# Branch products of a parallel mixer layer: two output blocks as seven block products

## The chip, the core and the metric

One core of one Trainium2 chip runs the kernel. The metric is the device time of one execution in microseconds (us). The kernel before takes 1344.15 us (median of three runs, 1344.06 to 1344.16).

## What is computed

One layer of an encoder on two groups of 512 tokens with the same weights, 1024 channels. Three attention branches A, B and C each give a state of 512 channels. The part that matters here is the merge of the three branches:

```
gates = jax.nn.sigmoid(mg).reshape(b, s, 3, D_MODEL)
m = gates[:, :, 0] * (ya @ wa) + gates[:, :, 1] * (yb @ wb) + gates[:, :, 2] * (yc @ wc)
x = x + rms_norm(m @ w_out, post_g)
```

Here `mg` is a product of the normed input with 3072 columns of the input weights, `ya`, `yb` and `yc` are the states, and `wa`, `wb`, `wc` are 512 x 1024. Everything is float32.

## The kernel before

Both groups are worked on together: 1024 tokens, channels on the partitions. TensorE multiplies numbers that are split in two parts, a rounded one (hi) and the rest (lo), and every product of two matrices is three matmuls: hi times hi, hi times lo, lo times hi. A matmul is a 128 x 128 block of weights against 128 x 512 numbers.

A weight block travels as follows. The queue of SyncE (SP) loads it from memory into one of the two slots of `stage` (`load_w`); ScalarE (ACT) writes the rounded part to `w_hi` (`split_w` at L1464); GpSimd (POOL) writes `stage` minus `w_hi` to `w_lo` (`split_w` at L666) and counts up `w_ready`; TensorE (PE) waits for that count. SP loads a block only when the split before it is done, and ACT writes a slot of `w_hi` only when PE is done with the block that was there. Blocks have numbers in one list over the whole program; a merge has sixteen of them, from `N_MERGE[b]`.

There are three merges, b = 0, 1, 2, one after each branch's attention. A merge alternates eight gate products and eight branch products. Gate product f (`merge_gate`, 48 matmuls at L843) makes 128 of the 1024 channels of a gate from the input; ACT takes its tanh. Branch product f (`merge_branch`, 24 matmuls at L1240: four blocks of 128 channels of the state, three parts, two groups) makes 128 channels of the projected state in banks 2 and 3 of PSUM (block 6: banks 0 and 1). VectorE (DVE) multiplies gate and product (`merge_add`, L2141 for b = 0; L2144 and L2146 for b = 1, 2, where it also adds to `m`) and counts up `merged`, which PE waits for before it writes these banks again. The order on PE is gate 0, gate 1, branch 0, gate 2, branch 1, gate 3, and so on; the last two are branch 6 and branch 7. The state's hi and lo parts, `y_hi` and `y_lo`, lie in `pt_hi` and `pt_lo`; DVE writes the lo part in `split_y` (L1981) just before a merge.

The order on each engine is the order of its code; nothing is scheduled. Behind merge 0 PE projects the first query block of branch B (`B_HEAD`, 24 matmuls at L1084, weights `N_B`) and then waits for `merged` before the first scores. Behind merge 1 it projects queries and keys of branch C (`N_C` and `N_C + 1`, 48 matmuls each at L843). Behind merge 2 comes the output projection (L1394). In merge 0, PE turns `rope_buf` (eight transposes at L870) ahead of branch 6.

Of the kernel before, what the change touches and what calls it, by code (L numbers as in the profile page):

```python
# [144 lines left out]
N_MERGE = [19, 42, 74]  # L145
N_B = 35
# [13 lines left out]
def build_program(nc, w_qkvg_a, w_qg_b, w_qkvg_c, w_gates, w_branch, w_out, w_pg, w_pe,  # L160
# [3 lines left out]
    with ExitStack() as ctx:  # L164
        def sb(name, shape, dt=F32):
            return ctx.enter_context(nc.sbuf_tensor(name, shape, dt))

        def sem(name):
            return ctx.enter_context(nc.semaphore(name))
# [7 lines left out]
        y = sb("y", [P, UNITS, TOK])  # L177
        q_hi = sb("q_hi", [P, TOK], F32R)
        q_lo = sb("q_lo", [P, TOK], F32R)
        k_hi = sb("k_hi", [P, TOK], F32R)  # L180
        k_lo = sb("k_lo", [P, TOK], F32R)
        v_hi = sb("v_hi", [P, TILES, 3 * HD], F32R)
        v_lo = sb("v_lo", [P, TILES, 3 * HD], F32R)
        vg = sb("vg", [P, TOK])
# [3 lines left out]
        tables = sb("tables", [P, 2 * NBIAS + ZW])  # L188
# [5 lines left out]
        spare = sb("spare", [P, TOK])  # L194
# [112 lines left out]
        merged = sem("merged")  # L307
        dve_step = sem("vector_step")
# [60 lines left out]
        v_plain_c = spare[:, 0:SEQ]  # L369

# [126 lines left out]
        def _(sp):  # L497
# [12 lines left out]
            def load_merge_rest(b):  # L510
                n = N_MERGE[b]
                with sp.Fori(0, KC - 2) as f:
                    load_w(n + 2 + 2 * f, n % 2, one(w_branch, b * KC + f))
                    load_w(n + 3 + 2 * f, (n + 1) % 2, one(w_gates, b * KC + 2 + f))
                for f in range(2):
                    load_w(n + 14 + f, (n + f) % 2, w_branch[b * KC + 6 + f])
# [87 lines left out]
            sp.wait_ge(maxed, LEAD + 24 * UNITS)  # L604
            for k in range(EARLY):
# [35 lines left out]
        def _(pool):  # L641
# [7 lines left out]
            for signal in (raw_used, bias_ready, x_pow, head_pow, y_pow, r_pow, b_pow, b_added, b_roped, w_ready, pool_step):  # L649
                pool.sem_inc(signal, LEAD)  # L650
# [17 lines left out]
            def split_merge(b, chunks):  # L668

                n, slot = N_MERGE[b], N_MERGE[b] % 2  # L670
                with pool.Fori(chunks.start, chunks.stop) as f:
                    split_w(n + 3 + 2 * f, 1 - slot)
                    split_w(n + 4 + 2 * f, slot, width=512)


# [46 lines left out]
            split_merge(0, range(1, KC - 2))  # L722
            split_w(N_MERGE[0] + 15, 0, width=512)
# [30 lines left out]
            split_merge(1, range(0, KC - 2))  # L754
            split_w(N_MERGE[1] + 15, 1, width=512)
# [40 lines left out]
            split_merge(2, range(0, KC - 2))  # L796
# [26 lines left out]
        def _(pe):  # L823
# [9 lines left out]
            for signal in (f_turned, x_turned, first_half, half_done, va_turned, rope_turned, bh_done, b_turned, b_back, scores, p_turned, p0_turned, mixed,  # L833
# [392 lines left out]
            def merge_branch(b, f, n, slot):  # L1226
# [5 lines left out]
                else:  # L1232
                    pe.wait_ge(merged, LEAD + b * KC + 1)
# [10 lines left out]

            def merge_rest(b):
# [1431 lines left out]
```

## Time and profile before

| what | us |
|---|---|
| median of three runs | 1344.15 |
| time of the profiled execution | 1343.39 |
| its span, first to last instruction | 1341.4 |
| PE busy, 6684 matmuls | 1322.7 |
| DVE busy | 602.4 |
| ACT busy | 551.9 |
| POOL busy | 301.7 |

The span leaves out what lies around the program, 2.0 us here. Busy time of PE is modelled at the end of each matmul, so the distance from one start to the next says more than a duration: a matmul is listed with 0.39 us, and the next one starts earlier than that.

### The profile page before, as it was taken

What the parts mean: (1) busy time and instruction counts of PE and PEld (TensorE: products, weight loads), DVE (VectorE), ACT (ScalarE), POOL (GpSimd) and SP (SyncE); (2) the same over time, 40 slices, a digit from 0 to 9 for tenths busy, and PEclk for the clock granted to TensorE, in tenths of its full rate; (3) what the DMA queues carried; (4) which work ended last, traced back from release to release, by engine and by line L of the source; (5) the groups of instructions that cost most, each with busy time, mean ns of one, the idle gap of its engine ahead of it and who ended that gap; (6) DMA issues with size and microseconds to landing.
All of it is one profiled execution on the core that took longest, in us unless ns stands there. A gap on an engine that the chain in (4) does not pass through costs nothing.

```text
span 1341.4 us, 17676 instructions
## 1 busy us (share of the span) xinstructions
PE 1322.7 (99%) x6684; PEld 1081.2 (81%) x6684; DVE 602.4 (45%) x1164; ACT 551.9 (41%) x1075; POOL 301.7 (22%) x199
## 2 busy tenths in 40 slices
PE   9999999999999999999999999999999999999998
PEld 6788778888888778888888888888877887888887
DVE  6355555555100477786311335555554115435222
ACT  6355554553111477676311145555553113223210
POOL 4121212221322311130222412221211222213100
PEclk9999999999999999999999999999999999999999
DMA  6111202111111100000111221111101113422111
GB/s 218 56 41 41 57 25 56 52 32 52 48 47 47 54 26 16 17 25 16 48 49 49 67 64 32 57 49 36 32 25 32 47 47 147 139 81 80 64 40 40
DMA packets 25836, 72.13 MB, mean 54 GB/s; under 512 B 2936, under 2 KB 4856, under 8 KB 25632
## 3 DMA queue, kind: packets, MB, share of 16 engines
q1 hardware_dynamic: 25760, 71.09, 16.8%
q8 instruction: 50, 0.82, 0.3%
q14 instruction: 26, 0.21, 0.0%
HBM read 66.86 MB, written 4.23 MB: 53 GB/s over the span
## 4 chain that ended last, share of the span: by engine, by line
PE 90%; DVE 4%; ACT 3%; DMA 1%; issue 1%; POOL 0%; SPq 0%; DVEq 0%; ACTq 0%; POOLq 0%
PE ps L843 18%; PE ps L862 14%; PE ps L1199 13%; PE ps L1240 9%; PE ps L1414 6%; PE ps L1084 6%; PE ps L1394 5%; PE ps L882 2%; PE ps L1021 2%; PE ps L937 2%; PE ps L1169 2%; PE ps L1420 2%; PE ps L1272 2%; PE ps L1052 1%; PE ps L1143 1%; PE ps L1119 1%
## 5 line engine op out<-in xcount | busy, mean ns | idle before, releaser
L666 POOL TENSOR_TENSOR w_lo<-stage,w_hi 128x1024 fp32r<-128x1024 f32 (+1 forms) x92 | 195.9, 2129 | 660.0 <-ACT w_hi L1464 660.0
L1464 ACT CAST w_hi<-stage 128x1024 fp32r<-128x1024 f32 (+1 forms) x92 | 86.3, 938 | 278.8 <-PE ps L843 197.6
L1981 DVE TENSOR_TENSOR pt_lo<-ps,pt_hi 128x512 fp32r<-128x512 f32 (+2 forms) x160 | 97.1, 607 | 80.5 <-ACT pt_hi L1795 40.4
L862 PE MATMUL ps<-h_hi,w_hi 128*128 128x512 f32 x272 | 110.3, 405 | 0.0
L843 PE MATMUL ps<-h_hi,w_hi 128*128 128x512 f32 x352 | 108.8, 390 | 0.0
L843 PE MATMUL ps<-h_hi,w_lo 128*128 128x512 f32 x352 | 108.4, 389 | 0.0
L843 PE MATMUL ps<-h_lo,w_hi 128*128 128x512 f32 x352 | 108.4, 389 | 0.0
L1199 PE MATMUL ps<-h_hi,w_hi 128*128 128x512 f32 x256 | 106.8, 417 | 0.0
L862 PE MATMUL ps<-h_hi,w_lo 128*128 128x512 f32 x272 | 106.2, 391 | 0.0
L862 PE MATMUL ps<-h_lo,w_hi 128*128 128x512 f32 x272 | 106.1, 390 | 0.0
L1199 PE MATMUL ps<-h_hi,w_lo 128*128 128x512 f32 x256 | 100.4, 392 | 0.0
L1199 PE MATMUL ps<-h_lo,w_hi 128*128 128x512 f32 x256 | 100.3, 392 | 0.0
L2144 DVE SCALAR_TENSOR_TENSOR s<-s,ps 128x1024 f32<-128x1024 f32 x15 | 18.3, 1220 | 149.5 <-PE ps L1240 149.5
L843 PEld LDWEIGHTS ps<-h_hi,w_lo 128*128 128x128 f32 x352 | 66.1, 188 | 13.8
L843 PEld LDWEIGHTS ps<-h_lo,w_hi 128*128 128x128 f32 x352 | 66.1, 188 | 13.8
L843 PEld LDWEIGHTS ps<-h_hi,w_hi 128*128 128x128 f32 x352 | 65.7, 188 | 14.1 <-issue 0.7
L647 POOL TENSOR_TENSOR small<-small 128x1 f32<-128x1 f32 (+3 forms) x32 | 34.1, 1067 | 173.8 <-DVE small L1996 173.0
L862 PEld LDWEIGHTS ps<-h_hi,w_hi 128*128 128x128 f32 x272 | 51.1, 188 | 15.1 <-issue 5.4
L1493 ACT ACTIVATE s<-s,stat 128x512 f32<-128x512 f32 x64 | 45.9, 719 | 38.2 <-DVE stat L2032 38.2
L1084 PE MATMUL ps<-h_hi,w_hi 128*128 128x512 f32 x144 | 59.8, 415 | 0.5 <-POOL w_lo L666 0.5
L862 PEld LDWEIGHTS ps<-h_hi,w_lo 128*128 128x128 f32 x272 | 51.1, 188 | 11.2
L1240 PE MATMUL ps<-pt_hi,w_hi 128*128 128x512 f32 x192 | 59.4, 390 | 0.0
(294 smaller groups left out, 2904.6 us busy)
## 6 DMA issues: line engine op xcount, KB each, us to landing
stage<-in_w_gates SPq DMA_DIRECT2D x24, 512.0 KB, 3.5
stage<-in_w_qkvg_a SPq DMA_DIRECT2D x19, 512.0 KB, 6.1
stage<-in_w_qkvg_c SPq DMA_DIRECT2D x16, 512.0 KB, 3.5
stage<-in_w_branch SPq DMA_DIRECT2D x24, 256.0 KB, 2.6
m<-in_x_tok SPq DMA_DIRECT2D x8, 512.0 KB, 8.2
y<-in_x_tok SPq DMA_DIRECT2D x8, 512.0 KB, 3.6
stage<-in_w_pg SPq DMA_DIRECT2D x16, 256.0 KB, 3.2
out<-y SPq DMA_DIRECT2D x16, 256.0 KB, 2.0
```

The lines of the kernel that those rows point to most:

```text
L647: nc.gpsimd.tensor_tensor(dst, src, neg_half.broadcast_to([P, n]), ALU.pow).then_inc(signal, 1)
L666: nc.gpsimd.tensor_tensor(dst, stage[:, staged, 0:width], f32(hi), ALU.subtract).then_inc(w_ready, 1)
L843: done = mm(ps[:, bank + g, :], w[:, slot, k * P:(k + 1) * P], h[:, k, g * SEQ:(g + 1) * SEQ], start=first and part == 0, stop=last and pa ...
L862: done = mm(ps[:, half_bank(T), :], w[:, slot, k * P:(k + 1) * P], h[:, k, g * SEQ:(g + 1) * SEQ], start=k == 0 and part == 0, stop=k == K ...
L1084: done = mm(ps[:, bank_b(name, unit, g), :], w[:, slot, k * P:(k + 1) * P], h[:, k, g * SEQ:(g + 1) * SEQ], start=k == 0 and part == 0, st ...
L1199: done = mm(ps[:, bank, :], w[:, slot, k * P:(k + 1) * P], h[:, k, g * SEQ:(g + 1) * SEQ], start=k == 0 and part == 0, stop=k == KC - 1 an ...
L1240: done = mm(ps[:, branch_bank(f) + g, :], w[:, slot, c * P:(c + 1) * P], yy[:, c * TOK + g * SEQ:c * TOK + (g + 1) * SEQ], start=c == 0 an ...
L1394: done = mm(ps[:, 2 * c + nb, :], a[:, k * P:(k + 1) * P], w[:, k, nb * 512:(nb + 1) * 512], start=k == 0 and part == 0, stop=k == KC - 1 ...
L1414: mm(ps[:, c, :], a[:, k * P:(k + 1) * P], w[:, k * 512:(k + 1) * 512], start=k == 0 and part == 0, stop=k == KC - 1 and part == 2)
L1464: nc.scalar.copy(dst, stage[:, staged, 0:width]).then_inc(w_hi_done, 1)
L1493: done = nc.scalar.activation(probs, probs, ACT.Exp, bias=stat[:, T % 2, 2 + e:3 + e], accum_out=stat[:, T % 2, 4 + e:5 + e])
L1981: sub = lambda out, whole, hi: nc.vector.tensor_tensor(out, whole, f32(hi), ALU.subtract)
```

## The change

Branch products of two neighbouring output blocks (a pair p: blocks 2p and 2p + 1) are made together. The pair of blocks, the two halves of the state's channels and the two groups of tokens form a 2 x 2 by 2 x 2 product, and Winograd's form of Strassen's scheme makes it of seven block products in place of eight. A block product is six matmuls (two blocks of 128 channels, three parts), so a pair is 42 matmuls in place of 48. Pairs 1, 2 and 3 are done so in merges 0 and 1, pairs 1 and 2 in merge 2 (`PAIRS`); blocks 0 and 1, and in merge 2 also 6 and 7, stay as they were. The scheme needs sums: four of the state for each merge (`state_sums` on DVE, split by ACT and by DVE in `state_lo`), four of the weights for each pair (on POOL, in `stage`, in place), and sums of the seven results (on DVE, in PSUM and in `partial`).

On PE a pair is `pair_first` (four block products into banks 0 to 3, 24 matmuls), a gate product, `pair_rest` (three block products into banks 0, 1 and 0, 18 matmuls), and a gate product; of pair 3 the two parts follow each other. SP loads both blocks of a pair with one DMA of 512 KB, where two of 256 KB were before. Loops over f are written out. Core of the diff:

```diff
+PAIRS = [range(1, KC // 2), range(1, KC // 2), range(1, KC // 2 - 1)]
+HALF_K = 2 * P
...
             def load_merge_rest(b):
...
+                for p in PAIRS[b]:
+                    sp.wait_ge(w_ready, LEAD + n + 4 * p + 1)
+                    pair = w_branch[b * KC + 2 * p:b * KC + 2 * p + 2].rearrange("a p n -> p a n")
+                    sp.dma_start(stage[:, n % 2, :].rearrange("p (a n) -> p a n", a=2), pair) \
+                        .then_inc(w_in_slot[n % 2], 16)
+                    if p < KC // 2 - 1:
+                        load_w(n + 4 * p + 3, (n + 1) % 2, w_gates[b * KC + 2 * p + 2])
+                        sp.wait_ge(w_ready, LEAD + n + 4 * p + 3)
+                        sp.sem_inc(w_in_slot[n % 2], 16)
+                        load_w(n + 4 * p + 5, (n + 1) % 2, w_gates[b * KC + 2 * p + 3])
+                    else:
+                        sp.wait_ge(w_ready, LEAD + n + 14)
+                        sp.sem_inc(w_in_slot[(n + 1) % 2], 16)
+                        sp.wait_ge(w_ready, LEAD + n + 16)
...
+            def split_pairs(b):
...
+                a11, a12, a21, a22 = [raw_w[:, q * HALF_K:(q + 1) * HALF_K] for q in range(4)]
+                split_w(n + 5, 1 - slot)
+                for p in PAIRS[b]:
+                    last = p == KC // 2 - 1
+                    pool.wait_ge(w_hi_done, LEAD + n + 4 * p + 3)
+                    steps.done(pool, nc.gpsimd.tensor_tensor(w_lo[:, slot, :], raw_w, f32(w_hi[:, slot, :]), ALU.subtract))
+                    nc.gpsimd.tensor_tensor(a22, a21, a22, ALU.add).then_inc(w_summed, 1)
...
+                    nc.gpsimd.tensor_tensor(w_lo[:, slot, 2 * HALF_K:3 * HALF_K], a22,
+                                            f32(w_hi[:, slot, 2 * HALF_K:3 * HALF_K]), ALU.subtract).then_inc(w_ready, 1)
+                    if not last:
+                        split_w(n + 4 * p + 3, 1 - slot)
+                    steps.done(pool, nc.gpsimd.tensor_tensor(a21, a11, a21, ALU.subtract))
+                    steps.done(pool, nc.gpsimd.tensor_tensor(a11, a22, a11, ALU.subtract))
+                    nc.gpsimd.tensor_tensor(a12, a12, a11, ALU.subtract).then_inc(w_summed, 1)
+                    pool.wait_ge(w_summed, LEAD + 2 * pair_number(b, p) + 2)
+                    if last:
+                        split_w(n + 15, 1 - slot, width=3 * HALF_K, staged=slot)
+                    else:
+                        split_w(n + 4 * p + 4, slot, width=3 * HALF_K)
+                        split_w(n + 4 * p + 5, 1 - slot)
...
+            def pair_first(b, p, n, slot):
+
+                pe.wait_ge(merged, LEAD + b * KC + 2 * p)
+                pe.wait_ge(w_ready, LEAD + n + 1)
+                pair_product(slot, 0, plain_state(0, 0), 0).then_inc(product_done, 1)
+                pair_product(slot, HALF_K, plain_state(1, 0), 1).then_inc(product_done, 1)
...
+            def pair_rest(b, p, n, slot):
+
+                number = pair_number(b, p)
+                pe.wait_ge(w_ready, LEAD + n + 1)
+                pe.wait_ge(p1_saved, LEAD + number + 1)
+                pair_product(slot, 0, T_PARTS[b][2], 0).then_inc(product_done, 1)
+                pe.wait_ge(bank1_used, LEAD + number + 1)
+                pair_product(slot, 2 * HALF_K, T_PARTS[b][3], 1).then_inc(product_done, 1)
+                pe.wait_ge(u2_saved, LEAD + number + 1)
+                pair_product(slot, HALF_K, plain_state(1, 1), 0).then_inc(block_done, 1)
...
+                def pair(p):
+                    number, last = pair_number(b, p), p == KC // 2 - 1
+                    raw_w = stage[:, slot, :]
+                    split_w(n + 4 * p + 2, slot, uses(4 * p + 2))
...
+                    act.wait_ge(w_summed, LEAD + 2 * number + 1)
+                    nc.scalar.copy(w_hi[:, slot, 2 * HALF_K:3 * HALF_K], raw_w[:, 3 * HALF_K:]).then_inc(s1_hi_done, 1)
...
+                        act.wait_ge(w_summed, LEAD + 2 * number + 2)
+                        split_w(n + 15, 1 - slot, uses(14), width=3 * HALF_K, staged=slot)
+                    act.wait_ge(product_done, LEAD + 4 * number + 1)
...
+                    nc.scalar.copy(partial[b][0], by_four(ps[:, 0, :])).then_inc(p1_saved, 1)
...
             merge(0)
-            split_w(N_B, 1, N_B // 2 + 1)
             act.wait_ge(rope_turned, LEAD + 2)
             q_to_hi(UNITS, 4)
+            split_w(N_B, 1, N_B // 2 + 1)
...
+                def pair(p, between_parts):
...
+                    dve.wait_ge(p1_saved, LEAD + number + 1)
+                    dve.wait_ge(product_done, LEAD + 4 * number + 2)
+                    steps.done(dve, add(bank(1), x0, bank(1)))
+                    add_quarter(2 * p, 0, 1).then_inc(bank1_used, 1)
...
+                    dve.wait_ge(product_done, LEAD + 4 * number + 3)
+                    add(x0, x0, bank(0)).then_inc(u2_saved, 1)
+                    dve.wait_ge(u2_saved, LEAD + number + 1)
+                    dve.wait_ge(product_done, LEAD + 4 * number + 4)
+                    steps.done(dve, add(x1, x0, bank(1)))
+                    add(bank(2), x1, bank(2))
+                    steps.done(dve, add(x0, x0, bank(3)))
+                    add(bank(3), x1, bank(3))
+                    dve.wait_ge(block_done, LEAD + (n + 16 if last else n + 4 * p + 5))
+                    steps.done(dve, add(bank(0), x0, bank(0)))
+                    add_quarter(2 * p, 1, 0).then_inc(merged, 1)
+                    add_quarter(2 * p + 1, 0, 2)
+                    add_quarter(2 * p + 1, 1, 3).then_inc(merged, 1)
```

`add_quarter` multiplies gate and result for 512 tokens; in merges 1 and 2 it is two instructions, of which the second adds two tiles in SBUF.

POOL at the end of merge 1 and the start of branch C, before: the body of its loop (two splits), the split for branch 7, and those for `N_C` and `N_C + 1`, behind which the bias tables of C are made.

```order
L666 TENSOR_TENSOR w_lo<-stage,w_hi 128x1024 [waits w_hi_done]
L663 REGISTER_ALU
L666 TENSOR_TENSOR w_lo<-stage,w_hi 128x512 [waits w_hi_done]
L671 REGISTER_ALU
L671 COMPARE_AND_BRANCH
L666 TENSOR_TENSOR w_lo<-stage,w_hi 128x512 [waits w_hi_done]
L666 TENSOR_TENSOR w_lo<-stage,w_hi 128x1024 [waits w_hi_done] x2
L766 TENSOR_TENSOR tables<-tables,mask 128x256 [waits raw_bias_in]
```

The same place after the change: gate 7's split, the split and the sums of pair 3, and then `N_C` and `N_C + 1`.

```order
L727 TENSOR_TENSOR w_lo<-stage,w_hi 128x1024 [waits w_hi_done]
L746 TENSOR_TENSOR w_lo<-stage,w_hi 128x1024 [waits w_hi_done]
L747 TENSOR_TENSOR stage<-stage 128x256 [waits gpsimd_step]
L750 TENSOR_TENSOR w_lo<-stage,w_hi 128x256 [waits first_weight_sum_hi_done,weight_sums_done]
L754 TENSOR_TENSOR stage<-stage 128x256
L755 TENSOR_TENSOR stage<-stage 128x256 [waits gpsimd_step]
L756 TENSOR_TENSOR stage<-stage 128x256 [waits gpsimd_step]
L727 TENSOR_TENSOR w_lo<-stage,w_hi 128x768 [waits w_hi_done,weight_sums_done]
L727 TENSOR_TENSOR w_lo<-stage,w_hi 128x1024 [waits w_hi_done] x2
L853 TENSOR_TENSOR tables_plain<-tables_plain,mask 128x256 [waits raw_bias_in]
```

The raw weights now stay in their slot of `stage` until the split of 768 columns, and `N_C` uses that slot next.

DVE at the start of merge 1, before: the lo part of the state, and then the first two outputs.

```order
L1981 TENSOR_TENSOR pt_lo<-y,pt_hi 128x1024 [waits y_hi_done] x4
L2144 SCALAR_TENSOR_TENSOR s<-s,ps 128x1024 [waits block_done,merge_tanh_done]
L2146 TENSOR_TENSOR m<-m,s 128x8x128 [waits vector_step]
L2144 SCALAR_TENSOR_TENSOR s<-s,ps 128x1024 [waits block_done,merge_tanh_done]
L2146 TENSOR_TENSOR m<-m,s 128x8x128 [waits vector_step]
```

After the change (a name with `_plain` is the same place under another type):

```order
L2146 TENSOR_TENSOR pt_lo<-y_plain,pt_hi 128x1024 [waits y_hi_done] x4
L2322 TENSOR_TENSOR k_hi_plain<-y_plain 128x512
L2323 TENSOR_TENSOR q_lo_plain<-y_plain 128x512 [waits vector_step]
L2324 TENSOR_TENSOR y_plain<-y_plain,k_hi_plain 128x512 [waits vector_step]
L2325 TENSOR_TENSOR y_plain<-y_plain 128x512 [waits vector_step]
L2322 TENSOR_TENSOR k_hi_plain<-y_plain 128x512
L2323 TENSOR_TENSOR q_lo_plain<-y_plain 128x512 [waits vector_step]
L2324 TENSOR_TENSOR y_plain<-y_plain,k_hi_plain 128x512 [waits vector_step]
L2325 TENSOR_TENSOR y_plain<-y_plain 128x512 [waits vector_step]
L2309 SCALAR_TENSOR_TENSOR s<-s,ps 128x1024 [waits block_done,merge_tanh_done]
L2311 TENSOR_TENSOR m<-m,s 128x8x128 [waits vector_step]
L2146 TENSOR_TENSOR y<-y_plain,y 128x2x512 [waits state_sums_hi_done] x2
```

Eight sums of two tiles in SBUF now stand between the state's lo part and the first output.

## Rows read from the trace of the kernel before

**Rows 1.** The page: busy time of the engines, and PE's granted clock in tenths.

```profile
PE 1322.7 (99%) x6684; PEld 1081.2 (81%) x6684; DVE 602.4 (45%) x1164; ACT 551.9 (41%) x1075; POOL 301.7 (22%) x199
...
PEclk9999999999999999999999999999999999999999
```

**Rows 2.** The chain in order of time, merge 0 and behind it: start, length, what.

```profile
335.45 5.44 PE ps L1240 x24
340.89 10.88 PE ps L843 x48
...
445.15 5.44 PE ps L1084 x24
```

**Rows 3.** Timeline of merge 0, from the end of a gate product: start, length, instruction.

```profile
335.29 0.62 PE L1240 MATMUL ps<-pt_hi,w_hi 128*128 128x512 f32 x2
335.55 1.05 ACT L1464 CAST w_hi<-stage 128x1024 fp32r<-128x1024 f32 x1 [7.14 <-PE ps L843]
...
336.67 2.40 POOL L666 TENSOR_TENSOR w_lo<-stage,w_hi 128x1024 fp32r<-128x1024 f32 x1 [12.27 <-ACT w_hi L1464]
...
339.24 0.33 SPq L501 DMA_DIRECT2D stage<-in_w_gates  x1
...
340.73 0.62 PE L843 MATMUL ps<-h_hi,w_hi 128*128 128x512 f32 x2
...
341.04 1.22 DVE L2141 SCALAR_TENSOR_TENSOR m<-s,ps 128x1024 f32<-128x1024 f32 x1 [7.40 <-PE ps L1240]
```

**Rows 4.** Groups by line and shape: instruction, count, busy us, mean ns, idle before.

```profile
L666 POOL TENSOR_TENSOR w_lo<-stage,w_hi 128x1024 fp32r<-128x1024 f32 x68 | 164.8, 2423 | 546.3 <-ACT w_hi L1464 546.3
L666 POOL TENSOR_TENSOR w_lo<-stage,w_hi 128x512 fp32r<-128x512 f32 x24 | 31.1, 1295 | 113.7 <-ACT w_hi L1464 113.7
...
L766 POOL TENSOR_TENSOR tables<-spare,mask 128x256 f32<-128x256 f32 x8 | 5.9, 735 | 0.0
...
L1464 ACT CAST w_hi<-stage 128x1024 fp32r<-128x1024 f32 x68 | 71.4, 1050 | 181.9 <-PE ps L843 161.3 <-PE ps L1240 16.5 <-DMA stage<-in_w_pe 4.1
...
L1464 ACT CAST w_hi<-stage 128x512 fp32r<-128x512 f32 x24 | 14.9, 623 | 96.9 <-PE ps L1240 60.6 <-PE ps L843 36.3
...
L1981 DVE TENSOR_TENSOR pt_lo<-ps,pt_hi 128x512 fp32r<-128x512 f32 x96 | 65.9, 687 | 42.8 <-ACT pt_hi L1795 40.4 <-ACT pt_hi L1508 2.1
...
L2330 DVE TENSOR_TENSOR tables<-tables 128x512 f32<-128x512 f32 x4 | 2.8, 689 | 0.1
```

**Rows 5.** Issues of the DMA queue: instruction, count, KB each, us to landing.

```profile
stage<-in_w_qkvg_a SPq DMA_DIRECT2D x19, 512.0 KB, 6.1
stage<-in_w_qkvg_c SPq DMA_DIRECT2D x16, 512.0 KB, 3.5
```

**Rows 6.** Timeline: PE behind a wait for DVE.

```profile
1132.95 0.70 PE L1394 MATMUL ps<-h_hi,q_hi 128*128 128x512 f32 x2 [1.83 <-DVE m L2146]
```

**Rows 7.** Timeline: DVE and POOL at work at the same time, and DVE alone.

```profile
440.93 2.41 POOL L666 TENSOR_TENSOR w_lo<-stage,w_hi 128x1024 fp32r<-128x1024 f32 x1 [5.47 <-ACT w_hi L1464]
...
441.81 1.22 DVE L2009 SCALAR_TENSOR_TENSOR q_lo<-ps,q_hi 128x1024 fp32r<-128x1024 f32 x1 [17.94 <-ACT q_hi L1467]
...
1129.34 5.72 POOL L666 TENSOR_TENSOR h_lo<-stage,h_hi 128x1024 fp32r<-128x1024 f32 x2 [7.00 <-ACT h_hi L1464]
1129.53 3.28 DVE L2146 TENSOR_TENSOR m<-m,s 128x1024 f32<-128x1024 f32 x1
...
1138.44 1.22 DVE L2146 TENSOR_TENSOR m<-m,s 128x1024 f32<-128x1024 f32 x1
```

**Rows 8.** Timeline: start of merge 1, DVE, POOL and PE.

```profile
644.34 4.62 DVE L1981 TENSOR_TENSOR pt_lo<-y,pt_hi 128x1024 fp32r<-128x1024 f32 x4
...
648.04 3.17 POOL L666 TENSOR_TENSOR w_lo<-stage,w_hi 128x1024 fp32r<-128x1024 f32 x1 [7.20 <-ACT w_hi L1464]
...
651.36 0.70 PE L843 MATMUL ps<-h_hi,w_hi 128*128 128x512 f32 x2
```

**Rows 9.** Timeline: the turn of `rope_buf` in merge 0.

```profile
433.22 1.03 PE L870 MATMUL ps<-ident,tables 128*128 128x128 f32 x8
```

More of the change, by code:

```diff
@@ L721, in _ @@
             inv_sqrt(head_rstd, head_ss, head_pow)
[L722 to L723 removed]
+            split_pairs(0)
             def split_b(k):
@@ L1243, in merge_branch, with pair_product, plain_state @@
                 done.then_inc(block_done, 1)
+            def pair_product(slot, first, state, bank):
+                hi, lo = state
+                for c in range(2):
+                    cols = slice(first + c * P, first + (c + 1) * P)
+                    for part, (w, h) in enumerate([(w_hi, hi), (w_hi, lo), (w_lo, hi)]):
+                        done = mm(ps[:, bank, :], w[:, slot, cols], h[:, c, :], start=c == 0 and part == 0,
+                                  stop=c == 1 and part == 2)
+                return done
+            def plain_state(k, g):
+                return state_half(y_hi, k, g), state_half(y_lo, k, g)
+            def pair_first(b, p, n, slot):
[3 more added lines that the diff above has]
+                pair_product(slot, HALF_K, plain_state(1, 0), 1).then_inc(product_done, 1)
+                if p == 1:
+                    pe.wait_ge(t_ready, LEAD + 4 * b + 1)
+                pair_product(slot, 3 * HALF_K, T_PARTS[b][4], 2)
+                if p == 1:
+                    pe.wait_ge(t_ready, LEAD + 4 * b + 4)
+                pair_product(slot, 2 * HALF_K, T_PARTS[b][1], 3).then_inc(block_done, 1)
+            def pair_rest(b, p, n, slot):
[7 more added lines that the diff above has]
+                pair_product(slot, HALF_K, plain_state(1, 1), 0).then_inc(block_done, 1)
             def merge_rest(b):
@@ new lines, in merge @@
+                split_w(n + 3, 1 - slot, uses(3))
+                merge_tanh(b, 1, n + 1, 1)
+                split_w(n + 4, slot, uses(4), width=512)
+                act.wait_ge(t_summed, LEAD + b + 1)
+                for k in T_ORDER[:3]:
+                    if b == 2 and k == 3:
+                        act.wait_ge(merged, LEAD + b * KC + 1)
+                    nc.scalar.copy(T_PARTS[b][k][0], T_SUMS[b][k]).then_inc(t_hi_done, 1)
+                split_w(n + 5, 1 - slot, uses(5))
+                merge_tanh(b, 2, n + 3, 0)
@@ L1706, in square_x @@
+                for p in PAIRS[b]:
+                    pair(p)
+                if KC // 2 - 1 not in PAIRS[b]:
+                    merge_tanh(b, 6, n + 11, 0)
+                    split_w(n + 14, slot, uses(14), width=512)
+                    split_w(n + 15, 1 - slot, uses(15), width=512)
+                    merge_tanh(b, 7, n + 13, 1)
             def square_x(t):
@@ L2169, in merge @@
-                merge_add(b, 7, n + 15, 1)
+                for j in range(3):
+                    state_lo(j)
+                merge_add(b, 1, n + 4, 1)
+                state_lo(3)
+                for p in PAIRS[b]:
+                    pair(p, before_6 if p == KC // 2 - 1 else None)
+                if KC // 2 - 1 not in PAIRS[b]:
+                    if before_6:
+                        before_6()
+                    merge_add(b, 6, n + 14, 0)
+                    if before_7:
+                        before_7()
+                    merge_add(b, 7, n + 15, 1)
```

206 lines of the change are left out of this document (143 added, 63 removed).

## The prediction

> **What bounds the kernel now.** I read the page first: PE is busy for 1322.7 of 1341.4 us at the full granted clock, the others for less than half [rows 1]. PE's busy time alone proves little, since its ends are modelled, so the chain in order of time comes next. In a merge it is PE without a break: 24 matmuls of a branch product in 5.44 us, 48 of a gate in 10.88, and so on [rows 2]. That is 0.2267 us from start to start, and the timeline confirms it: a branch product starts at 335.29 and the next gate at 340.73 [rows 3]. So the merges are bound by the number of matmuls, and a matmul that goes is worth 0.2267 us, as long as nobody makes PE wait. The rest of the reading is about who could.
>
> The handoffs come from the same stretch [rows 3]. When a gate product ends (335.29), ACT starts 0.26 later and rounds 1024 columns in 1.05; POOL follows after 0.07 and takes 2.40, so the lo part is there at 339.07; SP sends the next load 0.17 after that. DVE starts 0.31 after the end of a product (341.04 against 340.73). PE starts 0.14 after the DVE instruction that it waits for: that one began at 1129.53 and took 3.28, and PE started at 1132.95 [rows 6, 7].
>
> **What goes.** Eight pairs (three, three and two) of 42 matmuls in place of 48: 48 x 0.2267 = 10.88 us less. Six matmuls in a row now go into one bank where two banks took turns; the projection behind merge 0 puts 24 in a row into one bank and takes the same 5.44 [rows 2], so the pace stays. Each matmul loaded its weights anew before as well: 6684 loads for 6684 matmuls [rows 1].
>
> **What comes, where PE could wait.** I go through the waits in the order of a pair; M is the end of `pair_rest` on PE.
>
> Weights of the gate behind `pair_rest`. They can be split only when the gate before it is done, as before, but PE now gets there after 18 matmuls, 4.08 us, not after 5.44. The chain is 0.26 + 1.05 + 0.07 + 2.40 = 3.78, and 0.14 to PE: 3.92. It fits by 0.16, six times over (pair 3 has no such gate). I take nothing; if that cover goes, each 0.1 costs 0.6 in all.
>
> The third result has to be saved before the fifth matmul group of its bank: DVE sees it after 0.31, adds in 0.69 (an add from PSUM or SBUF takes 687 or 689 ns [rows 4]), 0.14 to PE: 1.14, against the six matmuls in between, 1.36. Nothing, eight times, with 0.22 to spare.
>
> DVE's work behind a pair: it sees the fourth result of the scheme at M - 1.05; then five adds and three quarters follow, in merge 0 eight instructions of 0.69, in merges 1 and 2 eleven. It ends at M + 4.5 or M + 6.5, plus up to 0.7 for a POOL instruction in the way. PE wants the banks after the next gate, at M + 10.88. At the end of merge 0 it wants them after the projection, M + 5.44; at the end of merge 1 the first C product uses another bank and the second starts at M + 10.88. Nothing. No instruction of DVE writes PSUM in this trace. I take 0.69 for these too, the price of the same add the other way; below that I see no reason to go, and at twice that only the end of merge 0 is late, by 4.5 + 3 x 0.69 - 5.44 = 1.1.
>
> POOL's added work before `pair_first` (the full split, one sum, the split of the sum: 0.26 + 1.05 + 0.07 + 2.42 + 0.74 + about 0.5 on ACT + 0.74 = 5.8, a sum of 256 columns at 735 ns [rows 4]) lies under a gate of 10.88. Its three other sums and the split of 768 columns (3 x 0.74 + 1.86) start when the gate's split is done, 3.8 after that gate's predecessor ends, and lie under 16.3 us of `pair_first` and gate. SP's one load per pair is sent during the gate before. ACT waits for POOL's sums with nothing urgent queued behind. All nothing.
>
> The end of merges 0 and 1. Here a cover does go. The raw weights of pair 3 hold their slot of `stage` until the split of 768 columns, and the next stage's first weights need that slot. Count from G, the end of gate 7. ACT starts at 0.26 and needs 0.84 for 768 columns (the middle of 1050 and 623 ns [rows 4]): 1.10. POOL: 0.07 + 1.86 (the middle of 2423 and 1295): 3.03. SP: 3.20. Landing: 3.5 for such a load [rows 5]: 6.70. ACT 1.05, POOL 0.07 + 2.42, PE 0.14: 10.38. PE has the two parts of pair 3 in between, 42 x 0.2267 = 9.52. In merge 1 it waits **0.86** for `N_C`. In merge 0 the turn stands in between, 0.8 to 1.0 us [rows 9], so that it waits for nothing. The landing is the uncertain part: 6.1 is the median of another load of that size [rows 5], which would add 2.6 at each place; a faster landing can give back 0.86.
>
> The start of merges. DVE now makes eight sums before the first output. Two things can be late. First, the output of block 0, which branch product 1 waits for: in merge 1 the sums can start at 651.2, when POOL is through its split [rows 8], take 8 x 0.72 and are held for 1.3 by POOL's next split; with two instructions of 1.22 for the output DVE is done at 660.7, and PE needs it at 651.36 + 10.88 = 662.2. Covered, by 1.5. Second, POOL itself: two-input instructions of DVE in SBUF and POOL's hold each other up. An add of 1.22 alone took 3.28 beside POOL's splits [rows 7]; and POOL's split at 648.04 took 3.17 in place of 2.40, because DVE was in its last `split_y` until about 648.9 [rows 8]. Gate 2's matmuls started right behind that split, at 651.36: there is no slack. If the first of the new sums gets in ahead of POOL, PE waits 0.69, in merges 1 and 2 (in merge 0 the split is done 1.5 before it is needed [rows 3]). POOL asked first, so it may cost nothing; the trace shows no queue of such sums behind a waiting POOL. I take half of 2 x 0.69: **0.69**.
>
> The sum, against the profiled execution of 1343.39: - 10.88 + 0.86 + 0.69 = 1334.06. The median lies 0.76 above that execution, which gives **1334.8**.
>
> **A rule on this.** In those rows DVE's 3.28 ends 1.07 after 1131.74, when the first of POOL's two instructions would end: the two engines took turns, each for one whole instruction, and DVE's subtraction from PSUM beside a POOL split took its usual 1.22 [rows 7]. The Trainium skill, SBUF — State Buffer, section Who interferes with whom, says just this: a DVE instruction with two SBUF inputs and a GpSimd instruction that reads SBUF exclude each other, the first to start blocks the other for the whole instruction, and a DVE instruction with at most one SBUF input is free of it. It speaks against the change, which gives both engines more of such work; by it alone, the place at the start of merges costs between nothing and 2 x 0.69, so 1334.1 to 1335.5.
>
> **Rivals.** First, **slower**: DVE's sums run as one block and POOL gets no turn in between. Then POOL's split for gate 2 starts only after all eight, 8 x 0.72 = 5.8 after 648.96; gate 2 starts at 657.3 in place of 651.36, 5.9 late, and the same in merge 2; in merge 0 DVE is free from 333.64 (7.40 idle before 341.04 [rows 3]), so POOL starts at 339.4 and the gate is 1.2 late. Together 13.0, less the 0.69 already counted: 1347.1. It beats the gain once POOL is held by 10 us in all. For it: no slack there. Against it: turns were taken [rows 7], and six of the eight sums wait for the one before, which leaves a gap. Chance 0.06.
>
> Second, **no change**: DVE's adds from PSUM are held by POOL as well. POOL splits the gate's weights from 1.38 to 3.78 after `pair_rest` starts, and DVE wants to save the third result at 1.67. It would then be saved at 4.47 and PE could go on at 4.61, not 2.72: 1.9, six times, 11.3 and a time of 1346.1. Against it: a subtraction from PSUM took 1.22 inside a split of 2.41 [rows 7]. Chance 0.05.
>
> Third, the seven products do not save the time of six matmuls, because their switching of banks, states and waits on PE costs it back: 0.1 at each of the 24 new waits is 2.4, a time of 1337.2; it needs 0.45 each to take all the gain. A boundary whose waits are over in time costs nothing visible now (340.73 lies on the grid of 0.2267 [rows 3]). This lies in the range; that it takes all has chance 0.03.
>
> **How the numbers follow.** The forecast has 0.86 with everything up to 1341.4. The range starts at 1333.0, the full 10.88 and a little for the spread of the runs, and ends at 1340.0, both landings at 6.1 (1334.8 + 5.1); 0.82 lies in it. What a measurement can tell from no change is 0.2%, 2.7 us: 1341.5 to 1346.8. Faster 0.86; within it 0.08 (the second and third rival); slower 0.06 (the first).
>
> **What the next profile would show.** 6636 matmuls; in the chain pieces of 24 and 18 matmuls in 5.44 and 4.08 with gates of 10.88; one wait of PE for POOL of some 0.9 at the start of branch C and none at the gates behind `pair_rest`; at gate 2 of merges 1 and 2 a wait for POOL of 0.7 or nothing; no wait of PE for DVE's adds. I am wrong where PE waits in every pair, for POOL behind `pair_rest` or for DVE within it, or where POOL's splits at the start of a merge are stretched by several us.

## The result and the profile after

The changed kernel takes 1334.53 us in the median of four runs (1333.35 to 1336.6), the kernel before 1344.11. The ratio is 0.9931 with a 95% interval of 0.9914 to 0.9949: 9.6 us less in the medians, and by the interval 6.9 to 11.6, with 1334.8 forecast. The profiled execution took 1336.60 us, the longest of the four, with a span of 1334.8, which is 6.6 less than the span before.

The page of the changed kernel, its line on busy time and PE's granted clock, answers to [rows 1]:

```profile
PE 1314.0 (98%) x6636; PEld 1073.2 (80%) x6636; DVE 681.8 (51%) x1285; ACT 575.5 (43%) x1106; POOL 350.8 (26%) x239
...
PEclk9999999999999999999999999999999999999999
```

There are 48 matmuls fewer, as the scheme says. DVE and POOL have 79 and 49 us more to do, which costs nothing by itself. The chain in order of time (start, length, what) shows a whole pair of merge 0, where [rows 2] had 24 and 48 in turn:

```profile
370.03 5.44 PE ps L1340 x24
375.47 10.88 PE ps L932 x48
386.35 4.14 PE ps L1340 x18
390.49 10.91 PE ps L932 x48
```

The third piece is the gain: 18 matmuls where 24 stood. For the whole program, the PE rows of the timelines give the length of each stage. A merge counts here from its first branch product to the first matmul behind it, so that a wait at its end belongs to it; the last column goes to the start of the last matmul. All in us:

| kernel | start | merge 0 | B | merge 1 | C | merge 2 | output |
|---|---|---|---|---|---|---|---|
| before | 335.29 | 109.69 | 200.72 | 109.14 | 267.01 | 111.10 | 203.51 |
| after | 337.23 | 105.84 | 200.67 | 106.06 | 267.03 | 108.53 | 204.48 |
| after, less before | +1.94 | -3.85 | -0.05 | -3.08 | +0.02 | -2.57 | +0.97 |
| again (the same kernel, below) | 335.77 | 105.80 | 200.57 | 105.96 | 267.10 | 108.52 | 204.23 |

The three merges together are 9.50 us shorter. The start and the output stage, which got longer, hold none of the changed products; they are taken up in the experiments. The waits of PE by line (us in all, times, longest) have one new entry, the first line here. Another has grown: PE's wait for DVE in the first 15 us, 2.2 where 0.3 stood, which is the late start of the table. The second line stood in before as well [rows 6]:

```profile
PE ps L932 <- POOL w_lo L727: 0.8, 1, 0.8
...
PE ps L1526 <- DVE m L2311: 1.8, 1, 1.8
```

The new one is the start of branch C, and the chain shows what it is made of. The raw weights of pair 3 leave `stage` with POOL's split (1.86), only then SP can load into the slot, and PE starts when the load has landed and has been rounded and split in its turn:

```profile
739.59 0.84 ACT w_hi L1596
...
740.56 1.86 POOL w_lo L727
...
742.44 3.68 DMA stage<-in_w_qkvg_c
...
746.14 1.06 ACT w_hi L1596
...
747.27 2.40 POOL w_lo L727
...
749.80 15.21 PE ps L932 x66
```

Inside a pair PE waits for nobody. The timeline around the first `pair_rest`, 386.19 to 390.33 (in brackets the idle time before):

```profile
386.45 1.05 ACT L1596 CAST w_hi<-stage 128x1024 fp32r<-128x1024 f32 x1 [9.60 <-PE ps L932]
...
387.57 2.42 POOL L727 TENSOR_TENSOR w_lo<-stage,w_hi 128x1024 fp32r<-128x1024 f32 x1 [8.75 <-ACT w_hi L1596]
387.75 0.69 DVE L2355 TENSOR_TENSOR m<-m,ps 128x512 f32<-128x512 f32 x1 [13.47 <-PE ps L1340]
...
389.93 0.69 DVE L2355 TENSOR_TENSOR ps<-m,ps 128x512 f32<-128x512 f32 x1
...
390.33 0.62 PE L932 MATMUL ps<-h_hi,w_hi 128*128 128x512 f32 x2
```

The split of the gate's weights ends at 389.99, and with 0.14 for the handoff PE could go on at 390.13; it gets there at 390.33. DVE's add from PSUM runs right through the split in its usual 0.69, and the add that writes PSUM takes 0.69 too. At the start of merge 1, which answers to [rows 8]:

```profile
646.07 3.18 POOL L727 TENSOR_TENSOR w_lo<-stage,w_hi 128x1024 fp32r<-128x1024 f32 x1 [7.21 <-ACT w_hi L1596]
646.92 2.88 DVE L2322 TENSOR_TENSOR k_hi_plain<-y_plain 128x512 f32<-128x512 f32 x1
...
649.40 0.47 PE L932 MATMUL ps<-h_hi,w_hi 128*128 128x512 f32 x1
```

The first sum of states is the one that waits (2.88 in place of 0.69), not POOL's split, which takes 3.18 as before (3.17). Gate 2 starts 5.66 after the branch product, as it did (5.65).

### The profile page after: what moved, and what is told of

Read it like the earlier page. It is cut to its first block, busy times and chain, and to the rows that moved or that the text cites. A ratio compares the mean times of both kernels' runs of the same rounds, so it can differ in the third digit from the quotient of the medians.

```text
span 1334.8 us, 17487 instructions
## 1 busy us (share of the span) xinstructions
PE 1314.0 (98%) x6636; PEld 1073.2 (80%) x6636; DVE 681.8 (51%) x1285; ACT 575.5 (43%) x1106; POOL 350.8 (26%) x239
## 4 chain that ended last, share of the span: by engine, by line
PE 91%; DVE 3%; ACT 3%; issue 1%; DMA 1%; POOL 0%; SPq 0%; ACTq 0%; DVEq 0%; POOLq 0%
PE ps L932 18%; PE ps L951 14%; PE ps L1288 13%; PE ps L1526 7%; PE ps L1546 7%; PE ps L1173 6%; PE ps L1340 5%; PE ps L1329 2%; PE ps L971 2%; PE ps L1110 2%; PE ps L1026 2%; PE ps L1258 2%; PE ps L1552 2%; PE ps L1404 2%; PE ps L1141 1%; PE ps L1232 1%
## 5 line engine op out<-in xcount | busy, mean ns | idle before, releaser
L727 POOL TENSOR_TENSOR w_lo<-stage,w_hi 128x1024 fp32r<-128x1024 f32 (+2 forms) x84 | 190.6, 2269 | 577.5 <-ACT w_hi L1596 577.5
L1596 ACT CAST w_hi<-stage 128x1024 fp32r<-128x1024 f32 (+2 forms) x92 | 91.3, 993 | 197.5 <-PE ps L932 126.1
L932 PEld LDWEIGHTS ps<-h_lo,w_hi 128*128 128x128 f32 x352 | 66.1, 188 | 13.9
L951 PEld LDWEIGHTS ps<-h_lo,w_hi 128*128 128x128 f32 x272 | 51.2, 188 | 9.3
L2468 DVE CUSTOM_DVE_ANT_0 s<-ps,tables_plain 128x256 f32<-128x256 f32 (+1 forms) x64 | 29.0, 489 | 56.3 <-PE ps L1232 51.9
```

The source lines that it names most:

```text
L727: nc.gpsimd.tensor_tensor(dst, stage[:, staged, 0:width], f32(hi), ALU.subtract).then_inc(w_ready, 1)
L932: done = mm(ps[:, bank + g, :], w[:, slot, k * P:(k + 1) * P], h[:, k, g * SEQ:(g + 1) * SEQ], start=first and part == 0, stop=last and pa ...
L951: done = mm(ps[:, half_bank(T), :], w[:, slot, k * P:(k + 1) * P], h[:, k, g * SEQ:(g + 1) * SEQ], start=k == 0 and part == 0, stop=k == K ...
L1596: nc.scalar.copy(dst, stage[:, staged, 0:width]).then_inc(w_hi_done, 1)
```

## The experiments

**The same kernel again.** The first profile had a late start and a stretch at half pace, and the question was what of that belongs to the change.

> The changed kernel once more, unaltered. In its first profile it showed three things besides the 48 matmuls: a start that was 1.9 us later than before's (the first gate product behind the state of merge 0 at 337.23, branch product at 335.29 in before), one PE wait of 0.81 at the start of branch C, and sixteen matmuls at half the pace behind the 1.82 us wait at the start of the output projection. My theory: the first is the scatter of the first loads and goes away (1332 to 1334 us without it), the second stays, the third comes and goes and costs 1.6 us where it is. Rival: the late start belongs to the change and comes back with the same 1.9 us.

Median 1334.27 us (1333.37 to 1335.27, five runs), ratio 0.9929 [0.9915, 0.9942]. The start came at 335.77, 0.48 late; the wait at C was 0.63 (0.79 from start to start); there was no stretch at half pace, but behind the first two tiles of the output projection a wait of 1.04 for DVE's `q_lo`, 0.33 in before. ACT, which feeds DVE there, had stood before a load:

```profile
1139.85 0.62 ACT L1596 CAST pt_hi<-stage 128x512 f32 x1 [7.71 <-DMA stage<-in_w_pg]
```

So the wait at C is the change's. The half pace comes and goes: this view of stretches (its length, busy time and count of each engine, granted clock, DMA share, GB/s) shows the same 3.5 us in the first profile and in this one:

```profile
1126.00:1129.50 3.50, 3.50 (x10) 2.76 (x9) 3.50 (x2) 0.00 (x0) 1.45 (x1) 0.52 0.00 0
```

```profile
1126.00:1129.50 3.50, 3.50 (x17) 2.89 (x16) 3.46 (x4) 0.00 (x0) 0.00 (x0) 1.00 0.12 19
```

PE is "busy" all the time in both, but with 10 matmuls in one and 17 in the other: the granted clock of 0.52 is the lower of its two levels (1.2 GHz), and PE had just stood still for 1.82 us. In the second, PE stood still for 1.81 at the same place and kept 2.4 GHz. The stretch holds eight matmuls that start some 0.427 apart (not the sixteen of the expectation) and cost 1.6 us, the sum of what they start later than at 0.2267 apart.

The start stays open in part. In the ten profiles with the changed code (here and below) it comes between 335.42 and 337.32, in two of the old code (before and before_out_late) at 335.29 and 335.17. In five of the ten, one of SP's first DMA issues takes 1.07 to 1.59 us where it took 0.42 to 0.51 in before, and all loads behind it come later. That is not the whole of it, since the latest start has no such issue. On average the ten start 1.1 later than the two, and the times scatter more as well: sets of 8 to 15 runs of the kernel before spread over 0.91 to 1.69 us, sets of 4 or 5 runs of the changed code (without sbuf_add below) over 1.18 to 3.25. So that the late start is mere scatter, as my theory had it, is not shown; what in the changed program could make it likelier was not tried.

**The slot of branch C's first weights.** SP loads them into the other slot of `stage`, free once gate 7's weights are split:

```diff
                         sp.sem_inc(w_in_slot[(n + 1) % 2], 16)
+                        if b == 1:
+                            sp.dma_start(stage[:, 1, :], w_qkvg_c[0]).then_inc(w_in_slot[1], 16)
                         sp.wait_ge(w_ready, LEAD + n + 16)
...
             for n in range(2):
-                split_w(N_C + n, n)
+                split_w(N_C + n, n, staged=1 - n)
```

> The first weights of branch C are loaded into the other slot of stage, which is free from the time gate 7's weights are split, so they no longer wait for the raw weights of pair 3. Theory: the wait of 0.81 (0.97 from start to start) at the start of branch C came from that slot alone. What is left is the chain behind pair_first: 0.26 + 1.05 + 0.07 + 2.42 + 0.14 = 3.94 against the 18 matmuls of pair_rest, 4.08. So the wait goes and the kernel is 0.97 us faster than the unaltered one. Rival: ACT or POOL is late there for reasons of their own (the sums, the tanh, DVE's m += s); then a wait of 0.5 or more for POOL stays and the time does not move.

The wait is gone. The load goes out at 726.37, 14 us earlier than the other weights', and PE starts 0.3 after POOL is through:

```profile
726.37 0.33 SPq L574 DMA_DIRECT2D stage<-in_w_qkvg_c  x1
...
743.15 1.05 ACT L1598 CAST w_hi<-stage 128x1024 fp32r<-128x1024 f32 x1 [2.62 <-PE ps L1342]
...
744.28 2.41 POOL L729 TENSOR_TENSOR w_lo<-stage,w_hi 128x1024 fp32r<-128x1024 f32 x1 [3.73 <-ACT w_hi L1598]
...
746.98 0.61 PE L934 MATMUL ps<-h_hi,w_hi 128*128 128x512 f32 x2
```

Merge 1 takes 105.06, 0.90 less than in again. The median, 1332.48, is 1.8 less; the profile has a shorter start (335.42) and output stage (202.87) as well, which this edit does not touch. My theory holds, with the size read from the stage.

**The wait at the output projection.** It is the old kernel's, but the half pace hangs on it.

```diff
+            pool.wait_ge(merged, LEAD + 3 * KC - 1)
             for k in range(2):
                 split_w(N_OUT + k, k, dst=h_lo[:, EARLY + k, :], hi=h_hi[:, EARLY + k, :])
```

> GpSimd splits the two last weights of the output projection only when DVE has added output 6 of merge 2. Theory: DVE's add into m (3.28 us, 1.23 alone) was held up by the first of these splits, since both read SBUF only; with the split behind it the add ends at 1123.17 and the PE wait of 1.82 us at the start of the output projection goes, at most 0.1 stays: 1.8 us faster, and no stretch of half pace behind it, which makes 3.4 us in the runs that had one. Rival: DVE gets there late anyway, or the splits, now 1.5 us later, make PE wait at the seventh row of weights (8.2 us into the projection): then PE loses 1 us or more there and the time stays.

DVE's add takes 1.22 here, 3.28 in before [rows 7], and PE starts at 1123.15, when its last branch product is through:

```profile
1121.70 1.22 DVE L2312 TENSOR_TENSOR m<-m,s 128x1024 f32<-128x1024 f32 x1
...
1123.01 6.65 POOL L727 TENSOR_TENSOR h_lo<-stage,h_hi 128x1024 fp32r<-128x1024 f32 x2 [8.48 <-DVE m L2312]
1123.15 0.62 PE L1527 MATMUL ps<-h_hi,q_hi 128*128 128x512 f32 x2
```

Merge 2 with the wait behind it takes 106.55, 1.97 less. Median 1332.24. The output stage shows no half pace; it has a wait of 0.31 for DVE 8.6 us into it. The same edit in the old kernel:

> The kernel before, with the one edit that GpSimd splits the two last weights of the output projection only when DVE has added output 6 of merge 2. Theory: the PE wait of 1.83 us at the start of the output projection is the old kernel's and has nothing to do with the change: merge 2 with the wait behind it takes 109.1 in place of 111.1 us, and the whole 1.9 us less, 1342.0. So the change's own gain is what stands between this kernel and the changed one with the same edit (out_late), some 9.8 us. Rival: the old kernel hides it elsewhere (the splits, now later, make PE wait at the seventh row of the weights): less than 1 us.

1341.08 us, ratio to before 0.9984 [0.9975, 0.9993], merge 2 with 109.11 in place of 111.10: 2 us that were to be had without the change. The gain between the two kernels with the edit is 8.8 in the medians and 9.8 in the merges (3.88, 3.38 and 2.56). The two were not run side by side: against the runs of the kernel before that were taken with each (1343.94 and 1343.46), one is 11.7 faster and the other 2.4, 9.3 apart. out_late's profile also started 2.1 later than before_out_late's.

**Both**, and then a third edit in the output stage:

> Both edits, the other slot for the first weights of branch C and the later splits of the output weights. Theory: they are independent, 0.97 + 1.8 = 2.8 us less than the unaltered kernel's undisturbed 1333.5, so 1330.7 us, and 13.4 less than before. Rival: one takes the other's gain (the wait at C only moves to the next weights of C): then not more than 1.8.

1331.80 us (1330.41 to 1332.46), ratio to before 0.9909 [0.9896, 0.9923]; merges of 105.84, 105.09 and 106.56, each as with one edit alone. The edits add up in the stages; the median is 2.5 below that of again, where 2.8 were expected. By the times alone this kernel can't be told from c_slot or out_late, whose intervals overlap with its own.

> The two edits of both, and a third one in the output stage: ACT squares a tile of the projection, and GpSimd takes its root, ahead of splitting the next weights of the gate (pg) instead of behind, so that neither queue waits for that load with the tile ready. Theory: the waits of PE for DVE's q_lo some 22 us into the output stage (1.04 in again, 1.23 in one_more, 0.29 in both) come from ACT, which stands in its queue before a load that lands 8 to 10 us after its issue; without that the output stage takes 203.0 us or a little less each time, 0.5 us less than both, about 1331.2, and the spread of the runs shrinks. Rival: the load is needed at that place anyway and the wait only moves: no change from both, or some 0.5 us more.

```diff
+                if not last:
+                    square_r()
                 split_w(N_PG[0] + 2 * i + c, c, N_PG[0] // 2 + i + 1,
                         dst=y_hi[:, bass.ds((2 * i + c) * 512, 512)], width=512)
...
-                act.wait_ge(r_done, LEAD + 2 * i + c + 1)
-                act.wait_ge(x2_ready, LEAD + 2 * i + c - 1)
...
+                if last:
+                    square_r()
```

1331.76 us, as both. The late wait for `q_lo` did not appear, nor had it in both: the 0.29 that the expectation counts there is another one, 8.6 us into the stage, and 0.27 of it stays. The output stage takes 203.37 against 203.59. The rival, no change, is what the time says, but the theory was not put to the test: none of the four profiles with the later splits has the wait, with or without this edit, while five of the eight others do (0.33 in before, 0.88 to 1.23 in four of the changed code). Whether the spread shrinks can't be told from four runs.

**The margin behind `pair_rest`.** Six gates that were said to be ready 0.16 early:

```diff
                         split_w(n + 4 * p + 4, slot, width=3 * HALF_K)
+                        pool.wait_ge(w_hi_done, LEAD + n + 4 * p + 6)
+                        steps.done(pool, nc.gpsimd.tensor_tensor(
+                            w_lo[:, 1 - slot, 0:HALF_K], stage[:, 1 - slot, 0:HALF_K],
+                            f32(w_hi[:, 1 - slot, 0:HALF_K]), ALU.subtract))
                         split_w(n + 4 * p + 5, 1 - slot)
```

> GpSimd does a quarter of the split of the gate's weights behind pair_rest twice (256 columns, 0.74 us and some 0.08 between two instructions), ahead of the split itself; the result is the same. Theory: the chain behind the end of the first gate of a pair is 3.94 us and PE has 4.08 to 4.14 us of work, so 0.2 of the 0.8 is hidden and PE waits 0.6 for POOL at six gates, two in each merge: merges of about 107.0, 107.2 and 109.7 us where the unaltered kernel has 105.8, 106.0 and 108.5, and 3.7 us more in all. Rival: POOL has slack there (PE needs the lo half of the weights only at the fifth matmul of the gate, 1.1 us later): no wait, the same time.

```profile
387.03 0.74 POOL L763 TENSOR_TENSOR w_lo<-stage,w_hi 128x256 fp32r<-128x256 f32 x1 [8.72 <-ACT w_hi L1600]
...
387.85 2.39 POOL L727 TENSOR_TENSOR w_lo<-stage,w_hi 128x1024 fp32r<-128x1024 f32 x1
...
390.39 0.70 PE L936 MATMUL ps<-h_hi,w_hi 128*128 128x512 f32 x2 [0.44 <-POOL w_lo L727]
```

PE now waits six times, 0.60 to 0.66 from start to start. POOL is 0.82 later, so 0.16 to 0.22 was hidden. Merges of 107.21, 107.48 and 109.86, 1338.54 us. The theory holds: POOL's chain is the next limit, and behind these 0.2 us there is no slack.

**What the operands of an add decide.** This was the second rival, which would have made the change worthless.

```diff
                     dve.wait_ge(product_done, LEAD + 4 * number + 3)
+                    steps.done(dve, add(x1, x0, x0))
                     add(x0, x0, bank(0)).then_inc(u2_saved, 1)
```

> In every pair VectorE does one add more, of two SBUF operands (128x512, 0.69 us), into a buffer that is free then, right ahead of the add from PSUM that saves the third result. Theory: an add with a PSUM operand runs beside GpSimd's split, one of two SBUF operands waits for the split to end. GpSimd starts its split 0.18 before VectorE gets there, so the added one starts 2.2 us late, the save ends about 3.65 us later than now instead of 0.72, and PE waits 2.6 us within seven of the eight pairs (at the end of merge 1 VectorE is first): 18 us more, merges of about 113.5, 111.5 and 113.7 us. Rival: the operands do not matter, only the add's own 0.72 us: PE waits 0.4 in each of eight pairs, 3.1 us more, merges of about 107.0, 107.2 and 109.3.

```profile
386.46 2.37 POOL L727 TENSOR_TENSOR w_lo<-stage,w_hi 128x1024 fp32r<-128x1024 f32 x1 [8.72 <-ACT w_hi L1596]
386.64 2.74 DVE L2355 TENSOR_TENSOR m<-m 128x512 f32<-128x512 f32 x1 [13.47 <-PE ps L1340]
...
389.42 1.41 DVE L2355 TENSOR_TENSOR m<-m,ps 128x512 f32<-128x512 f32 x2
...
390.16 0.51 PE L1340 MATMUL ps<-pt_hi,w_hi 128*128 128x512 f32 x1 [2.16 <-DVE m L2355]
```

The added instruction takes 2.74, of which all but 0.69 is the rest of POOL's split; the add from PSUM behind it takes its 0.69 again. PE waits seven times, 2.16 to 2.31 us, and 0.14 once. The time is 1355.07 us (1350.75 to 1357.37), 21 more than again where 18 were expected, and slower than before (ratio 1.0072 [1.005, 1.0094]). From start to start the waits are 2.33 to 2.48, seven of 2.33 are 16.3, and the one run with a mean granted clock of 1.0, 1350.75, is 16.5 above again. The rest is the clock: behind three of the seven waits, and again behind the 1.81 at the output projection, PE runs at half pace, as here behind the second one (columns as above):

```profile
424.00:427.30 3.30, 3.30 (x8) 2.62 (x9) 2.98 (x5) 0.34 (x1) 0.00 (x0) 0.51 0.00 0
```

Merge 0, with one such stretch, takes 114.81, merge 1, with two, 114.12, and merge 2, with none, 113.37 (113.7 expected). So what keeps the change cheap is that each add behind a product has one operand in PSUM. The Trainium skill, SBUF — State Buffer, section Who interferes with whom, draws the same line between one SBUF input and two, and these rows agree with it: 0.69 beside a split against 2.74.

**The sums of states without gaps.** The first rival had POOL locked out by eight sums in a row.

```diff
-                        steps.done(dve, nc.vector.tensor_tensor(t1, b12, b11, ALU.subtract))
-                        steps.done(dve, nc.vector.tensor_tensor(t3, b22, b12, ALU.subtract))
-                        steps.done(dve, nc.vector.tensor_tensor(t2, b22, t1, ALU.subtract))
...
+                    for t1, t2, t3, t4, b11, b12, b21, b22 in halves:
+                        nc.vector.tensor_tensor(t1, b12, b11, ALU.subtract).then_inc(steps.counter, 1)
...
+                    for c, (t1, t2, t3, t4, b11, b12, b21, b22) in enumerate(halves):
+                        dve.wait_ge(steps.counter, steps.base + steps.n + 3 + c)
+                        nc.vector.tensor_tensor(t2, b22, t1, ALU.subtract).then_inc(steps.counter, 1)
```

> VectorE does the eight sums of states in another order, the two halves in turn, so that no sum waits for the one before it and the eight follow each other without a gap. Theory: VectorE and GpSimd take turns whichever way the sums are queued; GpSimd, which asked for its split before the first sum could start, gets in after one instruction of VectorE at most, and merges 0, 1 and 2 take 105.8, 106.0 and 108.5 us as in the unaltered kernel, within 0.7 us each. Rival: GpSimd only got in because of the gaps between dependent sums; without them it waits for the whole block, up to 5.9 us at the second gate of merges 1 and 2 and 1.2 us in merge 0, 13 us more.

```profile
646.16 3.19 POOL L727 TENSOR_TENSOR w_lo<-stage,w_hi 128x1024 fp32r<-128x1024 f32 x1 [7.18 <-ACT w_hi L1596]
...
647.02 3.48 DVE L2325 TENSOR_TENSOR k_hi_plain<-y_plain 128x512 f32<-128x512 f32 x2
...
650.33 1.33 POOL L727 TENSOR_TENSOR w_lo<-stage,w_hi 128x512 fp32r<-128x512 f32 x1 [0.97 <-ACT w_hi L1596]
650.43 2.38 DVE L2327 TENSOR_TENSOR q_lo_plain<-y_plain 128x512 f32<-128x512 f32 x2
```

Both of POOL's splits get in between the sums, with 3.19 and 1.33 us (3.18 and 1.46 with the gaps). Merges of 105.81, 105.93 and 108.52: the same, so the turns do not need the gaps, and the rival falls. The second split shows it: ACT's rounding is done while one sum runs, and POOL gets in ahead of the next sum, which then takes 1.78 in place of 0.68.

**Without the last pair of merges 0 and 1.** In this kernel blocks 6 and 7 of these merges are multiplied with a state half that a sum has overwritten; the work is the same.

```diff
-PAIRS = [range(1, KC // 2), range(1, KC // 2), range(1, KC // 2 - 1)]
+PAIRS = [range(1, KC // 2 - 1), range(1, KC // 2 - 1), range(1, KC // 2 - 1)]
```

> Pairs of blocks 2 and 3 and of 4 and 5 only; blocks 6 and 7 of merges 0 and 1 are computed plainly as before, as those of merge 2 are anyway. That gives back 12 matmuls, 6 in each merge. Theory: merge 0 gets longer by 6 x 0.2267 = 1.36 us, less the 0.15 that its last pair loses by a slower pace, so 107.0; merge 1 by 1.36 less the 0.8 to 0.97 of the wait at the start of branch C, which goes with the pair's raw weights, so 106.5; merge 2 stays at 108.5; 1.7 us more in all. Rival: the wait at the start of branch C does not hang on that pair (it is there wherever DVE and GpSimd are late after a merge of pairs): merge 1 then takes 107.4, 2.6 us more in all.

Merges of 107.11, 106.53 and 108.51, each within 0.11 of the expectation (merge 0's 0.11 stands behind the turn, where the plain blocks lose 0.10 in the old kernel, too); 1336.24 us. PE goes into branch C without a wait:

```profile
745.88 2.40 POOL L727 TENSOR_TENSOR w_lo<-stage,w_hi 128x1024 fp32r<-128x1024 f32 x1 [4.58 <-ACT w_hi L1604]
...
749.94 0.62 PE L936 MATMUL ps<-h_hi,w_hi 128*128 128x512 f32 x2
```

So the wait hangs on that pair, and of the 1.36 us that the pair brings in merge 1 it leaves 0.57 (106.53 less the 105.96 of again).

## Why the prediction was right, step by step

**Matmuls, -10.88.** Right in number and in pace for `pair_first` (5.44) and for `pair_rest` in merge 1 (4.08). In merges 0 and 2 `pair_rest` took 4.14. The 42 matmuls of pair 3 in merge 0 took 9.67 where 9.52 is the old pace, but 0.10 of that was there before: behind the turn, the old kernel's 48 took 10.98. "So the pace stays" is therefore off by 0.23 in merge 0, 0.15 in merge 2 and some 0.03 in merge 1, 0.4 in all, most of it in `pair_rest` and a little in the gates behind. The timeline shows where it begins. The sum of states that the second block product of `pair_rest` reads lies in `vg` and `spare` in merge 0, in `spare` and `tables` in merge 2, and in `q_hi` and `q_lo` in merge 1. From the first matmul that reads `spare`, 11 take 2.55 us; the same 11 in merge 1 take 2.50, the old pace:

```profile
387.78 0.40 PE L1340 MATMUL ps<-spare,w_hi 128*128 128x512 f32 x1
...
390.33 0.62 PE L932 MATMUL ps<-h_hi,w_hi 128*128 128x512 f32 x2
```

```profile
725.91 0.39 PE L1340 MATMUL ps<-q_lo,w_hi 128*128 128x512 f32 x1
...
728.41 0.62 PE L932 MATMUL ps<-h_hi,w_hi 128*128 128x512 f32 x2
```

It begins at that matmul in every such pair of all ten profiles with the changed code. Whether it is the place of the sum, or something that goes with it, was not tried.

**The start of branch C, +0.86.** Measured 0.97 in the first profile and 0.70 to 0.96 in four others (0.40 in sbuf_add, where PE itself is late in that pair). Link by link from the end of gate 7 at 739.31: rounded at 1.12 (1.10 forecast), split at 3.11 (3.03), landed at 6.81 (6.70), PE at 10.49 (10.38). The landing, said to be the uncertain part, took 3.68, near the 3.5 of [rows 5] and far from 6.1. At the end of merge 0 the turn covered it: no wait, but with only 0.04 to 0.17 to spare in the eight profiles that have this pair and no added waits there.

**The start of merges 1 and 2, +0.69.** Measured nothing, at either. POOL had asked first and got its turn; the half that I charged stands for not knowing this from the trace of before. With sums_block the side is settled: there, too, POOL comes in ahead of a sum that stands in the queue.

**What was taken at nothing** stayed at nothing. The gates behind `pair_rest` were ready 0.16 early in merge 1, as forecast, and 0.20 to 0.21 in merges 0 and 2, where the slower pace adds to the margin. The third result was saved at 388.44 and PE wanted it at 388.94, so that 0.36 is left after the handoff (0.22 forecast). An add that writes PSUM takes 0.69, the value taken. In merge 1, DVE was through with the output of block 0 at 658.26, for a product at 660.38 (margin 2.1, 1.5 forecast). DVE's work behind a pair ended 4.1 us after `pair_rest` in merge 0 and 7.0 and 7.5 behind two pairs of merge 1 (4.5 and 6.5 to 7.2 forecast), for banks wanted at 10.88.

**The sum.** The merges were to lose 9.33 (10.88 - 0.86 - 0.69) and lost 9.50 in the first profile, 9.65 in again: the forecast of 0.69 too much and the pace of 0.4 too little nearly cancel. That the median lies within 0.3 us of the forecast is partly luck. The start (0.1 to 2.0 late in ten profiles) and the output stage (1.6 for half pace in two of the ten, 0.88 to 1.23 for a late load in four) move the single execution by more than any term but the first, and stood in no term.

**The rivals.** The slower one fell with sums_block. The second fell with the profile after, where the add from PSUM took 0.69 inside a split, and sbuf_add shows what it would have cost. Of the third (0.1 at each boundary, 2.4) 0.4 came, and not from the boundaries as such: `pair_rest` of merge 1 has the same banks and waits and keeps the old pace.

## What to carry to other kernels

Where one engine is busy without a break, a saved instruction is worth its spacing, and the work of a prediction is to walk every handoff that the shorter piece uncovers; a margin of 0.2 us holds when each link has a row. When two buffers' lives are lengthened by a change, look at who loads into them next: here the neighbour slot was free, and using it gave back the whole wait. Read a change of 1% stage by stage, since start and end of a program scatter by as much as one of its terms.

## What the runs showed of the hardware

A pause of PE can cost more than its length. Behind pauses of 1.81 to 2.31 us the granted clock fell to its lower level in some places (at the output projection in two of the eight profiles that have that pause, in sbuf_add behind three of seven others) and stayed at the higher one in the rest, with much the same work ahead of it; each time it fell it cost some 1.6 us more. What decides it, no run here shows. The spacing of matmuls can depend on more than their number and shape: 0.232 us in place of 0.2267 over 11 matmuls, from the first that reads `spare` on, with the cause open. And DVE and POOL share the reads of two SBUF operands in turns even when DVE's instructions stand in an unbroken row (in sums_block a split of 512 columns in the middle of the sums took 1.33 us, [rows 4] have 1.295), which I had thought might depend on the gaps.
